# Layer 0 takes its experts in the order of their counts, as layer 1 does

## The reference

```
scores = sigmoid(h @ router_w); sel = scores + router_bias
...  best group of 4 by its two largest, then its two best experts
for e in range(N_EXPERTS):
    a = jax.nn.silu(h @ w_gate[e]) * (h @ w_up[e])
    y = y + gates[:, e:e + 1] * (a @ w_down[e])
```

## The kernel before

| expert | 0 | 1 | 2 | 3 | 4 | 5 | 6 | 7 | 8 | 9 | 10 | 11 | 12 | 13 | 14 | 15 |
|---|---|---|---|---|---|---|---|---|---|---|---|---|---|---|---|---|
| rows, layer 0 | 67 | 29 | 70 | 8 | 18 | 103 | 56 | 81 | 46 | 42 | 151 | 77 | 92 | 48 | 51 | 85 |
| blocks, layer 0 | 3 | 1 | 3 | 1 | 1 | 4 | 2 | 3 | 2 | 2 | 5 | 3 | 3 | 2 | 2 | 3 |

## Time and profile before

### The profile page before, as it was taken

How to read it: one execution, slowest core, us unless ns; L and a number is a source line. 1 busy time by engine, 2 the same in 40 slices (tenths; PEclk the granted TensorE clock), 3 DMA queues, 4 the chain that set the end, 5 groups by cost and what they waited for, 6 DMA issues and landing times.

```text
span 1184.5 us, 24437 instructions
## 1 busy us (share of the span) xinstructions
PE 989.4 (84%) x9596; PEld 654.5 (55%) x9597; DVE 404.9 (34%) x809; ACT 374.9 (32%) x803; POOL 218.5 (18%) x329
## 2 busy tenths in 40 slices
PE   3799999978889989799899559999999779886650
PEld 1477777545555666457466447787555546553420
DVE  1533331357833531122122373222854512121103
ACT  3433221466621221122222344233852112221102
POOL 0000000000000024344344201910000224442211
PEclk8799999999989899899899969999999889998775
DMA  9766665998130658999999467224447699999972
GB/s 338 251 214 218 224 217 180 339 362 332 73 155 31 222 221 341 422 420 422 424 422 408 181 217 171 74 71 146 210 124 312 259 399 366 412 423 425 425 310 112
DMA packets 93682, 322.07 MB, mean 272 GB/s; under 512 B 21241, under 2 KB 33954, under 8 KB 81330
## 3 DMA queue, kind: packets, MB, share of 16 engines
q1 hardware_dynamic: 85746, 305.40, 66.7%
q0 software_dynamic: 7008, 12.62, 2.9%
q10 hardware_dynamic: 864, 3.15, 0.7%
HBM read 313.67 MB, written 13.99 MB: 277 GB/s over the span
## 4 chain that ended last, share of the span: by engine, by line
PE 65%; DMA 17%; DVE 7%; issue 4%; SPq 3%; ACT 2%; POOL 1%; DVEq 0%; POOLq 0%; ACTq 0%
PE ps L1878 24%; PE ps L1643 20%; DMA expert_sets<-in_moe_w_up_dram 10%; PE ps L1794 7%; PE ps L1546 4%; DMA ada_late<-in_ada_w_dram 3%; PE ps L1570 2%; DMA ring<-in_diff_w_qkv_dram 2%; SPq L608 1%; PE ps L1723 1%; PE ps L1752 1%; PE ps L1696 1%; SPq L590 1%; PE ps L1849 1%; DMA expert_rows<-moe,scatter_idx 1%
## 5 line engine op out<-in xcount | busy, mean ns | idle before, releaser
L1878 PE MATMUL ps<-expert_sets,moe 128*32 128x256 f32 x6304 | 369.9, 397 | 77.8 <-DMA expert_sets<-in_moe_w_up_dram 45.4
L1878 PEld LDWEIGHTS ps<-expert_sets,moe 128*32 128x32 f32 x6304 | 234.1, 115 | 212.9 <-issue 101.4
L1504 DVE STREAM_TRANSPOSE moe<-moe 128x256 f32<-128x256 f32 x70 | 46.0, 657 | 313.3 <-PE ps L1878 294.8
L1643 PE MATMUL ps<-w_high,x_high 128*128 128x512 f32 x352 | 143.5, 408 | 7.3 <-DVE hT L506 2.7
L1643 PE MATMUL ps<-w_high,x_low 128*128 128x512 f32 x352 | 139.8, 397 | 0.0
L1643 PE MATMUL ps<-w_low,x_high 128*128 128x512 f32 x352 | 139.6, 397 | 0.0
L473 DVE TENSOR_TENSOR w_low<-ring,w_high 128x2048 fp32r<-128x2048 f32 x24 | 58.0, 2424 | 131.4 <-ACT w_high L470 131.4
L743 POOL MEMSET moe<- 128x128 f32 x2 | 0.4, 206 | 548.6 <-PE ps L1820 548.6
L1068 ACT ACTIVATE moe<-ps 128x128 f32<-128x128 f32 x68 | 18.9, 278 | 259.7 <-PE ps L1878 257.5
L766 POOL DMA_INDIRECT expert_rows<-moe,scatter_idx x74 | 75.9, 1026 | 77.3 <-POOL scatter_idx L803 56.1
L1643 PEld LDWEIGHTS ps<-w_high,x_high 128*128 128x128 f32 x352 | 67.8, 192 | 32.0 <-issue 17.3
(11 more groups left out here) (235 smaller groups left out, 1118.9 us busy)
## 6 DMA issues: line engine op xcount, KB each, us to landing
expert_sets<-in_moe_w_down_dram SPq DMA_DIRECT2D x32, 2048.0 KB, 20.3
expert_sets<-in_moe_w_gate_dram SPq DMA_DIRECT2D x30, 2048.0 KB, 16.2
expert_sets<-in_moe_w_up_dram SPq DMA_DIRECT2D x30, 2048.0 KB, 21.2
ring<-in_ada_w_dram SPq DMA_DIRECT2D x16, 2048.0 KB, 8.0
ring<-in_diff_w_qkv_dram SPq DMA_DIRECT2D x6, 2048.0 KB, 8.1
ada_late<-in_ada_w_dram SPq DMA_DIRECT2D x6, 2048.0 KB, 11.8
ring<-in_na_w_qkv_dram SPq DMA_DIRECT2D x6, 2048.0 KB, 9.0
rows<-mod_rows SPq DMA_DIRECT2D x12, 512.0 KB, 8.6
```

Source lines behind the costliest of these rows:

```text
L1504: dve.transpose(blk_inT, blk_in[b].rearrange("p (j k) -> p k j", k=KC)).then_inc(m_xt[l], 1)
L1643: mm = pe.matmul(ps[:, n % 2], x_part[:, k, tok], w_part, start=(k == 0 and i == 0), stop=(k == KC - 1 and i == 2))
L1878: mm = pe.matmul(ps[g * SLOTS:(g + 1) * SLOTS, bank, 0:n_out], lhs_T[:, k, :], weights(k, g), start=(k == 0), stop=(k == n_chunks - 1), sk ...
```

## The change

Layer 0's branch of the plan, which took the experts by number, goes; layer 0 runs the code that was layer 1's. It is 13 operations of VectorE more in layer 0, and one more read of the plan by SyncE before each group of loads. The rule of the sort and the four fixed places are as in layer 1.

```diff
             def expert_at(l, p):
 
-                if l == 0:
-                    return p
                 return sp.value_load(plan[0:1, bass.ds(p + 2 + N_EXP, 1)], min_val=0, max_val=N_EXP - 1)
@@
-                cum = rt[:, 11, 32:32 + N_EXP] if l == 0 else moe[0:1, 3328 + 3 * N_EXP:3328 + 4 * N_EXP]
+                cum = moe[0:1, 3328 + 3 * N_EXP:3328 + 4 * N_EXP]
@@
-                if l == 1:
-                    key = rt[:, 6, 0:N_EXP]
-                    step(stt(key, total, float(N_EXP), const("sort"), ALU.mult, ALU.add))
...
+                key = rt[:, 6, 0:N_EXP]
+                step(stt(key, total, float(N_EXP), const("sort"), ALU.mult, ALU.add))
+                step(sooner(key))
+                step(dve.tensor_reduce(key, ahead, X_AXIS, ALU.add))
+                step(stt(key, key, -2 * MIDDLE, key, ALU.add, ALU.mult))
+                step(sooner(key))
                 off = (SLOTS - 1) / (2 * SLOTS)
                 rounded(nb, total, off)
                 step(ts(nb, nb, -ROUND, 1.0, ALU.add, ALU.max))
-                if l == 0:
-                    step(dve.tensor_tensor_scan(cum, nb, nb, 0.0, ALU.add, ALU.max))
-                    step(tt(base, cum, nb, ALU.subtract))
-                else:
...
+                step(tt(by_expert, ahead, nb.unsqueeze(1).to_broadcast([P, N_EXP, N_EXP]), ALU.mult))
+                step(dve.tensor_reduce(base, by_expert, X_AXIS, ALU.add))
@@
-                if l == 1:
...
+                step(dve.tensor_reduce(pos, is_at, X_AXIS, ALU.add))
+                step(tt(is_at, bcast(pos, 1), bcast(const("block")[0:1, 0:N_EXP], 2), ALU.is_equal))
+                step(tt(part_of, is_at, bcast(nb[0:1], 1), ALU.mult))
+                step(dve.tensor_reduce(blocks, part_of, X_AXIS, ALU.add))
+                step(tt(part_of, is_at, bcast(const("block")[0:1, 0:N_EXP], 1), ALU.mult))
+                step(dve.tensor_reduce(order, part_of, X_AXIS, ALU.add))
+                step(dve.tensor_tensor_scan(cum, blocks, blocks, 0.0, ALU.add, ALU.max))
+                step(dve.tensor_copy(plan[:, 2 + N_EXP:], order))
```

More of the change, by code:

```diff
@@ L1440, in _ @@
                 step(ts(nb, nb, -ROUND, 1.0, ALU.add, ALU.max))
-                if l == 0:
-                    step(dve.tensor_tensor_scan(cum, nb, nb, 0.0, ALU.add, ALU.max))
-                    step(tt(base, cum, nb, ALU.subtract))
-                else:
-                    step(tt(by_expert, ahead, nb.unsqueeze(1).to_broadcast([P, N_EXP, N_EXP]), ALU.mult))
-                    step(dve.tensor_reduce(base, by_expert, X_AXIS, ALU.add))
+                step(tt(by_expert, ahead, nb.unsqueeze(1).to_broadcast([P, N_EXP, N_EXP]), ALU.mult))
+                step(dve.tensor_reduce(base, by_expert, X_AXIS, ALU.add))
                 rank, full = ps[:, 4, 0:w], rt[:, 3, 0:w]
@@ L1476, in _, with bcast @@
                          slot_tab, ALU.mult, ALU.add), s_idx[l])
-                if l == 1:
[L1479 to L1492, removed]
+                pos, order, blocks = (moe[0:1, 3328 + i * N_EXP:3328 + (i + 1) * N_EXP] for i in range(3))
+                is_at, part_of = (t[0:1] for t in (ahead, by_expert))
+                def bcast(row, axis):
+                    return row.unsqueeze(axis).to_broadcast([1, N_EXP, N_EXP])
+                step(dve.tensor_reduce(pos, is_at, X_AXIS, ALU.add))
[6 more added lines that the diff above has]
+                step(dve.tensor_copy(plan[:, 2 + N_EXP:], order))
                 half_n = rt[0:1, 8, 0:1]
```

## The result

The changed kernel has a median of 1191.68 us (1189.43 to 1195.52, 6 runs) against 1186.13 for the kernel before on the same chips (6 runs): a ratio of 1.0043, interval 1.0027 to 1.0059. It is slower by some 5 us (5.1 by the ratio, 5.5 by the medians); 1183.8 was forecast, and the range ended at 1188. The profiled execution has a span of 1193.3 us; it is the slowest of the six (1195.52), 8.8 us above the span before.

What follows compares the result with a forecast made beforehand. Layer 0's expert stage was taken as bound by weight transfers, with TensorE nearly as full. The sum 0.6 + 1.7 - 5.2 + 1.2 - 0.4 = -2.1 us (-0.4: a last wait gone) gave 1183.8 us, range 1181 to 1188.

Steps and rivals of the forecast that it cites:

- Term 1: Layer 0's front: longer plan delays the third block, partly offset by a kept clock; +0.6 us, ends -0.9 and +3.3.
- the 1.1 us that I took back: Credit at the third block: TensorE idles 1.5 us, not 3.46, and keeps its clock; under half of 2.4 us.
- Term 2: Weight stream at place 7: its loads wait for place 4's five blocks, leaving a hole; +1.7 us, ends 0 and 2.7.
- Rival B: Slower: TensorE stalls entering place 4, the stream starves with a hole of 8.0 us; +3.0 us, 1188.9; chance 0.15.
- Term 3: Stage end: the last expert has two blocks for three, one block nearer the last up part's arrival; -5.2 us.
- Term 4: Stage end: TensorE idles before place 14, pays the slow clock and is late; +1.2 us, ends 0 and 2.4.
- Rival C: Nothing gained: the front passes with its full +3.3, the rest as forecast; -0.2 to +1 us, 1186; chance 0.20.
- faster: Whole kernel: the chance that the change makes it faster, put at 0.37, against same 0.46 and slower 0.17.

Runs made afterwards that it cites:

- e1: The changed kernel with sort constants that leave layer 0's experts in the order 0 to 15; 1192.02 us, ratio 1.0038 to the kernel before.
- e3: The program of e2 with the constants for the experts' order 0 to 15; 1188.38 us, ratio 1.0016 to the kernel before.
- e8: e3 with expert 10 (five blocks) moved to place 4; 1192.51 us, ratio 1.0045 to the kernel before.
- e2: The changed kernel's order in layer 0, but order and masks taken from constants, so the plan is shorter; 1188.56 us, ratio 1.0001 to the kernel before.
- e4: e3 with only places 14 and 15 exchanged, so the last expert has two blocks; 1186.76 us, ratio 1.0002 to the kernel before.
- e9: e2 with places 4 and 5 exchanged, the one-block expert before the five-block one; 1187.19 us, ratio 1.0010 to the kernel before.
- e5: The changed kernel with the extra up part issued only after three blocks' rows are transposed, both layers; 1185.87 us, ratio 0.9992 to the kernel before.
- e6: The kernel before with the extra up part issued only after three blocks' rows are transposed, both layers; 1183.17 us, ratio 0.9968 to the kernel before.
- e10: e1 with GpSimd's read of the plan moved behind its first four gathers, both layers; 1185.25 us, ratio 0.9986 to the kernel before.
- e7: The changed kernel with GpSimd's read of the plan moved behind its first four gathers, both layers; 1183.23 us, ratio 0.9971 to the kernel before.

## Why the prediction was wrong

**Term 1, the front, is the step that failed.** It was put at +0.6 us with ends at -0.9 and +3.3. Alone (e1) it measured 0.38%, 4.5 us, nine tenths of the 0.43% that the changed kernel lost. The lengths in it were right: +2.27, the half-clock product +0.6, and 3.15 for 3.07. What was wrong was one sentence, that the scatter "has at least a start" on the extra up part and so lands between 2.3 and 5.5 us later. The traces give:

| | extra part issued | first scatter issued | scatter landed | behind the extra part |
|---|---|---|---|---|
| before | 428.95 | 431.07 | 436.61 | 7.7 |
| e3 | 429.27 | 430.54 | 437.21 | 7.9 |
| e8 | 427.66 | 428.93 | 435.60 | 7.9 |
| after | 434.10 | 433.70 | 441.23 | 7.1 |
| e1 | 435.22 | 434.81 | 442.34 | 7.1 |

In e2, e4 and e9 the last column is 8.1, 8.0 and 7.9. The extra part itself landed 7.5 us behind its issue before, 7.6 after and 7.7 in e1. Whether the scatter is issued 2.1 us behind the 2 MB transfer or 0.4 us ahead of it, it lands when that transfer does, within 0.6 us in these three; alone it takes 2.15 to 2.4. So the third block was tied not to the scatter's own issue but to the extra part's, which waits for ScalarE's two copies, which wait for the plan. Nearly the whole delay passed: behind the ranks' product the plan was ready 6.0 us later, and the third block started 5.6 us later. That is beyond my upper end, since the 5.54 us belong to a scatter issued 2.1 us behind the transfer, and I took them for the worst case. And as TensorE then idled 4.63 us, not 1.5, the clock was at its lower level and the 1.1 us that I took back were not there. The scatter is not all of it: in e5 and e6, where it lands alone, the long plan still brings the first block and place 4's gate some 3.8 us later. That e10 (0.9986) is no slower than the kernel before does not make a long plan free, as the kernel before pays for its own scatter (e6 gains 3.8 us by freeing it); the kernel before with e10's edit was not run. Of the Trainium skill's rule that a DMA engine takes turns between its queues (DMA: Bandwidth & Descriptors, section Queues, rings and completion order) I said that the term is then near +3.3. It pointed the right way, that a head start is worth little; the 7.1 us go beyond the +3.3, and no run shows the turns.

**Term 2, the hole, was mis-sized.** It exists, at the place named, but place 7's gate came 59.1 us behind place 4's and not 57.2, because the first block behind the stall of 2.77 us at 486.48 ran at a granted clock of 0.60 and 0.55; in e7, behind a stall of 2.88 us, the clock stayed at 1.00, the same 576 matmuls took 31.29 us for 32.94, and the two gates are 57.3 us apart. I had priced no slow clock there. Ten loads and the 2.2 us make a hole of 3.6 us where 1.7 stood; the 0.58 share over 8 us says 3.4. e8 prices it as a whole at 3.4 us of the median and 5.4 of the stage. That no later hole was to be expected held here, by little: place 9's gate was issued at 545.20 with effect at 547.4, when the sixteen loads ahead, late by the first hole, ran until 548.6 by 5.55 us a load, and the DMA share is 0.98 and 1.01 from 544 to 552. In e9, without the first hole, the same count leaves one of 2.7 us. Rival B had this mechanism and another cause, a long stall at TensorE's entry into place 4; the stall in front of place 4 is 2.77 us for 2.83 before, and 576 matmuls follow without a gap. The stall of 3.91 us that stood behind place 4 has moved behind place 5, now the expert of one block, as 1.39 and 2.19 us (520.81, 527.05), which the prediction had under B; why one block brings it, no run isolates.

**Term 3, the last expert, was right in size.** Place 15's blocks end 13.0 us after they start (the last down at 676.07, the first block's transposition at 666.70 less 3.66), against 18.9 before. e4 is the exchange of the last two alone: 1.7 us by the ratios, and 3.9 of stage, of which 2.1 were there before the programs part. It is less than 5.2 because TensorE, and no longer the last up part, then sets the end.

**Term 4** stood at +1.2 and came at about 1.8: three loads behind 644.55 is 661.2, and place 15 began near 663.0. The wait before place 14, 4.99 us for some 6, and the slow clock behind it are as forecast.

**The sum by the changed kernel's rows**: third block and place 4's issue +4.7, hole +3.6, a slower pace of the remaining loads (644.55 - 515.3 over 23 loads is 5.62 each, and so 1.6 in all, whose cause is open), TensorE late +1.8, last expert -5.9, together +5.8, where the last down came 6.0 later. The terms of the order alone give about +1, not -2.7; by the ratios the order is worth -1.8 us between e7 and e10 and between e2 and e3, and +0.6 between the changed kernel and e1. Each of these three differences lies within its uncertainty. Rival C, the front passing in full with no net gain, was the nearest of those I named, and its price was too low by the same sentence. In the prediction's numbers the parts given for "faster" make 0.35, not 0.37; nothing hangs on it.

Not settled: why e7 gained 8.5 us where the third block came 4.3 us earlier. The profile of e7 shows two slow stretches of the clock less, in the third block (10.57 us for 12.25) and at place 4 (the hole smaller by 1.8 us); with the 4.3 that is 7.8 of the 9.2 by which its stage is shorter, and the rest I can't place. Nor is it clear what of the changed kernel's execution at 1195.52 belongs to it: layer 1's first transposition was 6.1 us late and its last down 8.9.

## What to carry to other kernels

When a step is delayed, ask which transfer is tied to the same delay. Here a small transfer that met a 2 MB one ended when the large one did, a lead of 0.4 us did not help it, and moving either out of reach of the other gave 3.8 to 8.5 us. In a stage whose weights come in one saturated stream, the order of the work does two things above all: it decides when buffers come free (count the blocks until each release against the loads still ahead, for every release, not just for the first) and how much is left to do behind the last arrival. Put the smallest piece last, and no long one where the stream's lead is short. And set a gain read from one profiled execution beside the medians: two programs alike up to a point can be 2 us apart there by the clock alone.

## What the runs showed of the hardware

A 128-row indirect scatter takes 2.15 to 2.4 us alone and ends 7.1 to 8.1 us after the issue of a 2 MB load that is issued between 2.1 us before and 0.4 us after it (eight kernels), about when that load lands (7.5 to 7.7); a gather issued 4 us behind such a load took 5.11 us for 2.5. A product of 64 small matmuls took 1.56 us after 3.18 us of idleness, for 0.92 us after 0.90; after 4.63 us the granted clock stood at 0.50, the lower level of 1.2 GHz, in the next block, as after 3.46 us before. Between 2.7 and 3.1 us it went either way: low after 2.77 (the changed kernel, 0.60), 2.90 (e5, 0.50) and 2.93 (e3, 0.50), at 1.00 after 2.83 (before), 2.88 (e7) and 3.08 (e10).
